# Norm factors as exponential of minus half the logarithm, turned memory between attention-out tiles, second out unit rounded later

## The reference

```
# first block
h = rms_norm(x, g);  proj = h @ w_in            # conv input, q, k, v, gates
conv_out = silu(layer_norm(depthwise_conv31(a * sigmoid(gate))))
q = rms_norm(q) ; k = rms_norm(k)               # per head half of 64 columns
a = softmax(q1 k1) - lam * softmax(q2 k2);  o = a @ v
attn_out = rms_norm(o, subln_g) * 0.8           # per head of 128 columns
merged = gates0 * (conv_out @ w_conv_out) + gates1 * (attn_out @ w_attn_out)
x = x + merged @ w_out
x = x + moe(rms_norm(x))                        # 32 experts, 2 per token
# second block
x = x + mixers(rms_norm(x)) @ w_out_2
x = x + cross_attention(rms_norm(x), rms_norm(mem))
x = x + conv_ffn(rms_norm(x));  out = rms_norm(x)
```

## Time and profile before

| | |
|---|---|
| three runs | 1039.8, 1040.21, 1042.54 us, median 1040.21 |
| profiled execution | 1040.6 us |
| its span, first to last instruction | 1038.8 us |
| TensorE busy | 906.6 us (87%) |
| VectorE busy | 458.1 us (44%) |
| ScalarE busy | 350.5 us (34%) |
| mean granted TensorE clock | 0.941 |
| moved by DMA | 301.27 MB, mean 290 GB/s |
| chain that ended last | TensorE 59%, DMA 27%, VectorE 8%, ScalarE 3% |

### The profile page before, as it was taken

The page is one execution under the profiler, slowest core; times in us unless marked ns, Lnnn a source line. Parts: engine busy times, 40 slices in busy tenths (PEclk is TensorE's granted clock), DMA queues, the critical chain, the costliest instruction groups (busy, mean ns, idle before and its releaser), DMA issues.

```text
span 1038.8 us, 14337 instructions
## 1 busy us (share of the span) xinstructions
PE 906.6 (87%) x6040; PEld 659.7 (64%) x6040; DVE 458.1 (44%) x804; ACT 350.5 (34%) x561; POOL 8.0 (1%) x14
## 2 busy tenths in 40 slices
PE   8999999999889947858775766999999989999997
PEld 7969878955246411313222131488999989999886
DVE  6899858511010010100101010188656676988752
ACT  5453483311010000100000010349565645756542
POOL 1000000000000000000000000000100000000000
PEclk9999999999999987978888896999999999999999
DMA  9866434989999999999999999982524245664451
GB/s 332 295 224 228 178 122 170 393 338 420 415 411 426 382 429 423 426 425 425 429 418 432 421 428 425 404 290 82 166 101 160 86 158 163 198 206 166 168 197 41
DMA packets 78493, 301.27 MB, mean 290 GB/s; under 512 B 4195, under 2 KB 30948, under 8 KB 62818
## 3 DMA queue, kind: packets, MB, share of 16 engines
q1 hardware_dynamic: 76640, 298.82, 73.0%
q10 hardware_dynamic: 1458, 1.07, 0.4%
q0 software_dynamic: 336, 0.53, 0.3%
HBM read 298.84 MB, written 1.05 MB: 289 GB/s over the span
## 4 chain that ended last, share of the span: by engine, by line
PE 59%; DMA 27%; DVE 8%; ACT 3%; issue 1%; SPq 1%; DVEq 0%; ACTq 0%
PE bank L1412 11%; DMA ring<-in_w_gate_e_dram 9%; DMA ring<-in_w_down_e_dram 8%; PE bank L1079 8%; DMA ring<-in_w_up_e_dram 7%; PE bank L1430 6%; PE bank L1303 3%; PE bank L1318 3%; PE bank L781 3%; PE bank L1137 3%; PE bank L688 2%; PE bank L715 2%; DVE big L1971 2%; DMA qvpr<-in_w_down_e_dram 2%; PE bank L1109 2%; PE bank L955 2%
## 5 line engine op out<-in xcount | busy, mean ns | idle before, releaser
L1079 PE MATMUL bank<-ring,big 128*32 128x512 f32 x768 | 163.9, 711 | 76.5 <-DMA ring<-in_w_up_e_dram 38.6
L1079 PEld LDWEIGHTS bank<-ring,big 128*32 128x32 f32 x768 | 38.8, 127 | 193.8 <-issue 90.1
L352 DVE TENSOR_TENSOR ring_parts<-ring,ring_parts 128x2048 fp32r<-128x2048 f32 (+1 forms) x54 | 118.8, 2248 | 35.9 <-ACT ring_parts L344 35.5
L344 ACT ACTIVATE ring_parts<-ring 128x2048 fp32r<-128x2048 f32 (+1 forms) x53 | 96.6, 1874 | 55.5 <-DMA ring<-in_w_up_dram 26.1
L2261 DVE TENSOR_TENSOR xT<-bank,xT 128x512 f32<-128x512 f32 x32 | 22.1, 692 | 137.0 <-PE bank L1123 137.0
L1412 PE MATMUL bank<-mrg_parts,ring_parts 128*128 128x256 f32 x640 | 82.3, 281 | 0.0
L1412 PEld LDWEIGHTS bank<-mrg_parts,ring_parts 128*128 128x128 f32 x640 | 78.5, 189 | 0.0
L2218 DVE TENSOR_TENSOR big<-big,const 128x128 f32<-128x128 f32 x14 | 3.5, 289 | 154.4 <-PE bank L1066 154.4
L1079 PE MATMUL bank<-hs,big 128*32 128x512 f32 x128 | 67.8, 683 | 0.0
L1109 PE MATMUL bank<-ring,big 128*32 128x512 f32 x336 | 45.8, 673 | 18.9 <-DMA ring<-in_w_down_e_dram 16.8
L1079 PE MATMUL bank<-qvpr,big 128*32 128x512 f32 x112 | 60.7, 696 | 0.6 <-DMA qvpr<-in_w_gate_e_dram 0.6
(11 more groups left out here) (423 smaller groups left out, 1627.3 us busy)
## 6 DMA issues: line engine op xcount, KB each, us to landing
ring<-in_w_up_e_dram SPq DMA_DIRECT2D x24, 2048.0 KB, 28.8
ring<-in_w_gate_e_dram SPq DMA_DIRECT2D x24, 2048.0 KB, 22.4
ring<-in_w_down_e_dram SPq DMA_DIRECT2D x17, 2048.0 KB, 21.5
ring<-in_w_in_dram SPq DMA_DIRECT2D x12, 2048.0 KB, 14.2
ring<-in_w_up_dram SPq DMA_DIRECT2D x22, 1024.0 KB, 7.2
ring<-in_w_down_e_dram SPq DMA_DIRECT2D x12, 1024.0 KB, 20.3
ring<-in_w_down_dram SPq DMA_DIRECT2D x5, 2048.0 KB, 7.9
ring<-in_w_out_dram SPq DMA_DIRECT2D x4, 2048.0 KB, 9.8
```

The costliest lines, as they stand in the source:

```text
L344: signal(act.activation(pairs[stage][u % 3][0][:, part], raws[stage][u % 3][:, part], ACT.Copy), stage + "_hi")
L352: signal(eng.tensor_tensor(lo[:, part], raws[stage][u % 3][:, part], hi[:, part].bitcast(F32), ALU.subtract), name)
L1079: mm = pe.matmul(bank[part][CAP * j:CAP * j + CAP, :], xeT[:, c, CAP * j:CAP * j + CAP], w[j][c], start=(c == 0), stop=(c == DC - 1))
```

## The change

Keys and queries: ScalarE takes the logarithm of each mean square and then the exponential of minus half of it, so that it delivers the inverse root itself; VectorE's reciprocals go. `queries_and_keys` and the rests of gate unit 2 are taken inside the convolution of chunks 2 and 3, ahead of its step 6 (five taps after the first), and the maxima stay at the middle tap.

Heads: the same two functions, now ahead of the memory's squares and root on ScalarE. On VectorE both products come ahead of the memory's small reciprocal, and the gated tiles behind them.

Turned memory: TensorE turns it after attention-out tiles 0 to 3 and before tiles 4 to 7, and the list of bank uses has the same order.

Second out unit: ScalarE rounds it after the eight merged tiles instead of before.

One semaphore is dropped (its two steps count on another) and one added, `root_inv`.

```diff
-    uses += some("co", 4, 5) + some("on", 0, 2) + some("co", 5, 8) + some("mT", 0, 4) + some("ao", 0, 8) + [("rb", 0)] + some("wo", 0, 4) + some("rt", 0, 2) + some("wo", 4, 8)
+    uses += some("co", 4, 5) + some("on", 0, 2) + some("co", 5, 8) + some("ao", 0, 4) + some("mT", 0, 4) + some("ao", 4, 8) + [("rb", 0)] + some("wo", 0, 4) + some("rt", 0, 2) + some("wo", 4, 8)
...
             for m in range(5, 8):
                 linear(("co", m), w_conv, m, big[:, 16 * T:20 * T], 4)
-            pe.wait_ge(S["mem_root"], 6)
-            for i in range(4):
-                turn(("mT", i), [(c * T + t * P, memtok[:, t, (2 * i + c) * P:(2 * i + c + 1) * P])
-                                 for c in range(2) for t in range(TT)])
+
+            def turned_memory():
+
+                pe.wait_ge(S["mem_root"], 6)
+                for i in range(4):
+                    turn(("mT", i), [(c * T + t * P, memtok[:, t, (2 * i + c) * P:(2 * i + c + 1) * P])
+                                     for c in range(2) for t in range(TT)])
 
...
                     if half:
                         filled(mm, ("ao", m))
+            turned_memory()
             for m in range(4, 8):
                 linear(("ao", m), w, m, qko[:, 8 * T:12 * T], 4)
...
-                read = {("var", 0): ("qk_ready", 1), ("on", 0): ("conv_z", 4), ("on", 1): ("qk_ready", 2),
-                        ("nmix", 0): ("attn_out", 2), ("nffn", 0): ("normed", 16)}
+                read = {("var", 0): ("qk_ready", 1), ("nmix", 0): ("attn_out", 2), ("nffn", 0): ("normed", 16)}
...
             for t in range(TT):
                 move(("v", t), vtok[:, 512 * t:512 * t + 512], 512)
-            b = arrive(act, ("qn", 0))
-            emptied(act.activation(q_root, b[:, 0:16], ACT.Sqrt, bias=EPS, scale=1.0 / 64), ("qn", 0))
+            def inverse_roots(names, dsts, n):
+
+                for use, r in zip(names, dsts):
+                    b = arrive(act, use)
+                    emptied(act.activation(r, b[:, 0:r.shape[1]], ACT.Ln, bias=EPS, scale=1.0 / n), use)
+                for use, r in zip(names, dsts):
+                    copied(act, use)
+                    signal(act.activation(r, r, ACT.Exp, scale=-0.5), "root_inv")
+
+            inverse_roots((("kn", 0), ("kn", 1), ("qn", 0)), (rs2[1], rs2[0], q_root), 64)
             move(("lam", 0), st[:, 102:104], 2)
-            for i in range(2):
-                root(("kn", i))
             round_gates(2)
             gates(0, 4)
...
             square(qko[:, 2048:3072], sq[:, 0:1024], 1024)
+            act.wait_ge(S["qk_ready"], 2)
+            inverse_roots((("on", 0), ("on", 1)), (rs2[1], rs2[0]), P)
             act.wait_ge(S["mem_in"], 16)
             for t in range(TT):
                 signal(act.activation(qko[:, D * t:D * t + D], memtok[:, t], ACT.Square, accum_out=mem_sq[:, t:t + 1]), "mem_root")
             act.wait_ge(S["mem_root"], 2)
             signal(act.activation(mem_r, mem_sq, ACT.Sqrt, bias=EPS, scale=1.0 / D), "mem_root")
-            root(("on", 0))
-            root(("on", 1))
             act.wait_ge(S["mem_root"], 4)
             for t in range(TT):
                 signal(act.activation(memtok[:, t], memtok[:, t], ACT.Copy, scale=mem_r[:, t:t + 1]), "mem_root")
...
-            arrive(act, ("gt", 15))
-            round_out(1)
             for m in range(DC):
                 act.wait_ge(S["merged"], m + 1)
                 signal(act.activation(mrg_hi[:, m * T:m * T + T], mrg[:, m * T:m * T + T], ACT.Copy), "mrg_hi")
+            arrive(act, ("gt", 15))
+            round_out(1)
             square_residual("wo", sq)
...
-            signal(act.activation(f_e, f_abs, ACT.Exp, scale=-1.0), "f_exp")
-            act.wait_ge(S["f_exp"], 1)
-            signal(act.activation(f_e, f_e, ACT.Ln, bias=1.0), "f_exp")
+            signal(act.activation(f_e, f_abs, ACT.Exp, scale=-1.0), "g_exp")
+            act.wait_ge(S["g_exp"], 3)
+            signal(act.activation(f_e, f_e, ACT.Ln, bias=1.0), "g_exp")
...
-            def convolve(ms, between=None, tap=CW // 2):
+            def convolve(ms, between=()):
 
                 y = {m: big[:, (16 + m) * T:(17 + m) * T] for m in ms}
                 last = {m: signal(dve.tensor_scalar(y[m], rows[:, m, 0:T], col("taps", CW * m), col("conv_b", m),
                                                     ALU.mult, ALU.add), "dve_step") for m in ms}
                 for j in range(1, CW):
-                    if j == tap and between:
-                        between()
+                    for tap, work in between:
+                        if j == tap:
+                            work()
                     for m in ms:
...
                 for i in range(2):
-                    r = inverse_root(("kn", i))
+                    dve.wait_ge(S["root_inv"], i + 1)
+                    r = rs2[TURN[("kn", i)]]
                     x = qko[:, 1024 + 512 * i:1024 + 512 * i + 512]
                     signal(dve.scalar_tensor_tensor(out=x, in0=x, scalar=qk_gain, in1=r, op0=ALU.mult, op1=ALU.mult), "qk_ready")
-                copied(dve, ("qn", 0))
-                step(dve.reciprocal(q_root, q_root))
+                dve.wait_ge(S["root_inv"], 3)
                 signal(dve.tensor_scalar(q_scale, q_root, 0.125, None, ALU.mult), "dve_step")
                 step(dve.tensor_scalar(q_neg, q_root, -0.125, None, ALU.mult))
...
             rest_of_gates(0)
             rest_of_gates(1)
-            queries_and_keys()
-            rest_of_gates(2)
-            convolve((2, 3), first_maxima)
+
+            def keys_and_gates():
+                queries_and_keys()
+                rest_of_gates(2)
+
+            convolve((2, 3), ((6, keys_and_gates), (CW // 2, first_maxima)))
...
             gated_conv(range(4))
             gated_conv(range(4, 5))
-            dve.wait_ge(S["mem_root"], 3)
-            signal(dve.reciprocal(mem_r, mem_r), "mem_root")
             for i in range(2):
-                r = inverse_root(("on", i))
+                dve.wait_ge(S["root_inv"], 4 + i)
+                r = rs2[TURN[("on", i)]]
                 x = qko[:, 2048 + 512 * i:2560 + 512 * i]
                 for h in range(2):
                     copied(dve, ("o1", 2 * i + h))
                 signal(dve.scalar_tensor_tensor(out=x, in0=x, scalar=st[:, 105:106], in1=r,
                                                 op0=ALU.mult, op1=ALU.mult), "attn_out")
-                if i == 0:
-                    gated_conv(range(5, 8))
+            gated_conv(range(5, 6))
+            dve.wait_ge(S["mem_root"], 3)
+            signal(dve.reciprocal(mem_r, mem_r), "mem_root")
+            gated_conv(range(6, 8))
 
             def rest_of_out(u):
```

More of the change, by code:

```diff
@@ L228, in two_blocks_kernel @@
         names = """x_hi x_lo in_hi in_lo h1_hi h1_lo ff_hi ff_lo pair_used h_hi h_lo up_val act_hi act_lo ident_in const_in par_in x_in x2_in g1_in small_in n1_root n1_diag mem_in out_done dve_step act_step zeroed squares normed lam_in
-                   sq_sums qk_ready s_max s_exp a_ready conved conv_dev conv_z conv_sig mem_root n2_inv out_hi out_lo mrg_hi mrg_lo x_gain mix_sum mix_hi mix_lo post_hi post_lo s_inv conv_out attn_out merged
+                   sq_sums qk_ready root_inv s_max s_exp a_ready conved conv_dev conv_z conv_sig mem_root n2_inv out_hi out_lo mrg_hi mrg_lo x_gain mix_sum mix_hi mix_lo post_hi post_lo s_inv conv_out attn_out merged
                    logits g_exp member rounds picked pick_step hid_step swt_full rows_full swt rows gate_sig
-                   hidden hid_full hidT y_out comb_full added pos_f ang trig rope rows_zero f_abs f_exp
+                   hidden hid_full hidT y_out comb_full added pos_f ang trig rope rows_zero f_abs
                    keys_early keys_read keys_in keys_full keys_out spare_in half_used down_early value_early w_first_in xq_hi xq_lo xq_sum gate_hi xq_scale gate_lo gain_in down_half last_half last_sum last_root vx_full vx_out c_rows z_pool y_mix up_conv up_sig""".split()
@@ L2339, in _ @@
             step(dve.tensor_scalar(f_z, f_z, 0.0, None, ALU.min))
-            dve.wait_ge(S["f_exp"], 2)
+            dve.wait_ge(S["g_exp"], 4)
             step(dve.tensor_tensor(f_z, f_z, f_e, ALU.subtract))
```

## The result

The changed kernel takes 1043.01 us (median of 20 runs, 1040.33 to 1044.07), the one before 1040.15 (20 runs). Their ratio is 1.0019, interval 1.0012 to 1.0027: slower by 2.0 us (1.2 to 2.8). The forecast had the change 0.55 us faster; the median lies above the prediction's range (1037.5 to 1042.4), 2.9 us over the median before. By the ratio alone the changed kernel would be at 1042.1, just inside. The profiled execution took 1043.06 us, with a span of 1041.3.

The account below looks back on a forecast made before the run. Expert weights set the pace, so TensorE's arrival there was taken to shift the end one to one. A net 0.55 us, 0.45 of it from the keys, off the 1040.21 us median gave 1039.7 us, range 1037.5 to 1042.4.

Parts of the forecast that it names:

- Ln load 1.28: 145.1: Heads' norm on ScalarE: the logarithm's table load follows the squares ending at 143.8, takes 1.28 us and ends at 145.1.
- Tile 4 starts at 161.4 ... 1.9 us of TensorE's idle time are back, in one piece: Attention-out: tile 4 waits 1.9 us for VectorE to empty tile 0's bank, starting at 161.4 against 161.94 before.
- rival three: TensorE's clock falls behind the 1.9 us gap after the turned memory, costing 1.7 us: 1041.4 us; chance 0.12.
- the gain of 0.45 us at the means: Convolution's means: TensorE no longer waits for the last taps, taking 1.89 instead of 2.34 us.
- the 6.8 us that VectorE then idles before the first maxima: VectorE at the second convolution's middle tap: about 6 us lost waiting for TensorE's first scores, from 92.1 to 98.1.
- two loads for each pair of functions: ScalarE, keys and heads: one table load before the logarithms and another before the exponentials, 1.28 us each.
- both waits of attention-out gone: TensorE at attention-out: neither half waits for its normalised heads; the second half's wait had been 1.24 us.
- the second out unit hidden: Rounding the second out unit after the merged tiles costs nothing; its rests keep 3 us of cover before TensorE needs them.
- a shift at the first out unit that reaches the end: Expert stage: any shift of TensorE's arrival reaches the end one to one, as weight loads wait for buffers TensorE frees.
- Rival two: One table load serves logarithm and exponential, tile 4 starts at 160.1: 1.8 us gained in all, 1038.4 us; chance 0.09.
- Rival four: Each table switch holds ScalarE longer than its load; two at the heads cost 2.6 us more: 1042.3 us; chance 0.03.
- Rival one: The gain stays because tile 4 does not wait for VectorE: 2.5 us earlier, 1037.7 us; chance 0.10.

Follow-up runs that it names:

- load early: Changed kernel with ScalarE's wait for the keys moved ahead of the squares of the heads; 1.0003 of the kernel before, 1.7 us under the changed kernel.
- second trace: The changed kernel profiled once more as it is, with no edit; 1045.53 us in that execution.
- Turned twice: Changed kernel with the memory's 16 transposes done twice, ahead of the same wait for tile 0's bank; 1.0002 of the kernel before.
- products first: Changed kernel with VectorE's products and sums of attention-out tiles 0 to 3 ahead of the first out unit's rests; 1037.96 us, 0.9974 of the kernel before.
- heads as before: Changed kernel with the heads' square roots and reciprocals, and the memory's squares ahead of them, as in the kernel before; 1.0010 of the kernel before.

## Why the prediction was wrong

Counted from the values, the forecast had tile 4 at 161.4 less 57.40 = 104.0 us; it is at 163.61 less 58.67 = 104.94, where the kernel before had 104.54. The first out unit was forecast 0.55 us earlier than before; 0.94 us of the first step below and 1.6 us of the second make that the 2.0 us later of the first trace. Two steps failed.

- **"Ln load 1.28: 145.1".** I let the load run as soon as the squares were done. It stood behind the wait for TensorE's sums and began 0.98 us later, and with it the first out unit's rounding (4.0 us later than before, where 3.0 was forecast). With the load early the gap is 0.9 us shorter, which is this term. The rest of the chain was sized well: logarithms 1.09, exponentials 1.15 for 1.06 each, and a crossing of 0.23 us from VectorE's small reciprocal to the scaled copies.
- **"Tile 4 starts at 161.4 ... 1.9 us of TensorE's idle time are back, in one piece", at the old clock.** The bank, the releaser and the place were right. That I priced the gap at its length was the main error: the clock behind it cost another 1.6 us in one trace and 3.0 in the other. It was rival three, with 1.7 us as its price and a chance of 0.12; that its price comes near the first trace's 1.6 us is luck, as the second trace's 3.0 shows. The mechanism was in the rows (0.57 over 198 to 202 us); I held it unlikely because two short gaps in the same place had left the clock at 1.00. Turned twice shows the clock's share by itself, products first that of gap and clock together (4.7 us, against 2.97 and 1.6 in the first trace).

What held: the gain of 0.45 us at the means (in every trace with the keys' part, the heads' sums come 86.3 us after the values, against 86.7), the 6.8 us that VectorE then idles before the first maxima, two loads for each pair of functions, both waits of attention-out gone, the second out unit hidden, and a shift at the first out unit that reaches the end, over a range of 6.6 us in the table. One to one holds to within 1 us there (load early, 1.3 and 0.3, is the furthest off, apart from the changed kernel's second trace with 3.4 against 2.0), and the 1.0 us of the router's stage, there or not, is of the same size.

```profile
DVE att L1904 <- PE bank L715: 6.8, 1, 6.8
```

Rival two (one load) is false in this kernel: the loads at 77.02 and 148.43. Rival four (a switch holds ScalarE for longer than its load) is false too: the load at 148.43 ends at 149.71, and the exponentials start at 149.72. Rival one was false for the change as made, and is what the products first make true: 2.7 us under the kernel before, where it had 2.5.

## What to carry to other kernels

When a change brings work forward on the critical engine, follow the banks: moving four uses in a round-robin plan changed which reader had to be done before tile 4, and the reader stood behind 4.4 us of work that TensorE wanted only later. Put what empties a bank ahead of such work. And price TensorE's idle time twice, once for its length and once for the slower work behind it; one long gap can cost more than two short ones of the same sum (2.97 us with a fall of the clock in three traces, 2.10 and 1.31 us without one in heads as before).

## What the runs showed of the hardware

- A gap of 2.07 to 4.96 us in front of float32 matmuls was followed by work at about half clock (the granted clock fell to 0.50 to 0.63 in the stretches behind it), worth 1.5 to 3.0 us each time, in five traces; 1.22 us was not, and 2.10 us in another place was not. Where the border lies, and what else it hangs on, is open.
- A table load takes its place among the waits: with one wait ahead of the function it ran while the engine would have waited (keys, 73.22, the sums came 0.97 us after its end); behind two waits it began only when both were over (heads, 146.03). With the first of the two moved ahead of the squares it ran right behind these (load early, 145.55).
